# Latent attention with four heads' query columns in three weight units

## The reference

```python
q = (_rmsnorm(q_lat, g_q_lat[i]) @ w_q_up[i]).reshape(bsz, s, N_HEADS, QK_DIM)
kv = (_rmsnorm(kv_lat, g_kv_lat[i]) @ w_kv_up[i]).reshape(bsz, s, N_HEADS, NOPE_DIM + V_DIM)
q_nope, q_pe = q[..., :NOPE_DIM], q[..., NOPE_DIM:]
k_nope, v = kv[..., :NOPE_DIM], kv[..., NOPE_DIM:]
q_pe = _rope(q_pe, positions)
k_pe = _rope(k_rope[:, :, None, :], positions)
q_full = jnp.concatenate([q_nope, q_pe], axis=-1)
k_full = jnp.concatenate([k_nope, jnp.broadcast_to(k_pe, (bsz, s, N_HEADS, ROPE_DIM))], axis=-1)
ob = _chunk_causal_attention(q_full, k_full, v).reshape(bsz, s, N_HEADS * V_DIM)
```

## Time and profile before

| | before |
|---|---|
| median of 3 runs | 1703.1 us (1702.91 to 1703.26) |
| profiled execution | 1703.2 us |
| its span | 1701.4 us |
| mean granted TensorE clock | 0.997 of full |

### The profile page before, as it was taken

How to read it: one execution, slowest core, us unless ns; L and a number is a source line. 1 busy time by engine, 2 the same in 40 slices (tenths; PEclk the granted TensorE clock), 3 DMA queues, 4 the chain that set the end, 5 groups by cost and what they waited for, 6 DMA issues and landing times.

```text
span 1701.4 us, 22070 instructions
## 1 busy us (share of the span) xinstructions
PE 1687.1 (99%) x7852; PEld 1403.8 (83%) x7852; DVE 951.1 (56%) x1637; ACT 610.5 (36%) x1160; POOL 974.8 (57%) x595
## 2 busy tenths in 40 slices
PE   9999999999999999998999999999999999999998
PEld 8788888888888888887888888888888888888887
DVE  7877422156642554155767454438657967775244
ACT  5455311243221222144733322322523137765022
POOL 6656566665666666754755555546564663333654
PEclk9999999999999999998999999999999999999999
DMA  5222222222222222223222222222232221111222
GB/s 209 83 70 79 91 95 99 99 88 99 91 104 103 99 99 99 99 99 99 87 87 75 75 89 97 75 74 87 87 107 75 100 87 50 50 51 62 88 91 82
DMA packets 52424, 152.26 MB, mean 89 GB/s; under 512 B 11376, under 2 KB 12528, under 8 KB 52336
## 3 DMA queue, kind: packets, MB, share of 16 engines
q1 hardware_dynamic: 51472, 149.50, 25.5%
q10 hardware_dynamic: 864, 1.57, 0.3%
HBM read 148.95 MB, written 2.10 MB: 89 GB/s over the span
## 4 chain that ended last, share of the span: by engine, by line
PE 97%; DVE 2%; issue 1%; ACT 0%; POOL 0%; DVEq 0%; POOLq 0%
PE bank L867 28%; PE bank L868 28%; PE bank L869 28%; PE bank L1716 1%; PE bank L1314 1%; PE bank L1315 1%; PE bank L1318 1%; PE bank L1556 1%; PE bank L1555 1%; PE bank L1559 1%; PE bank L905 1%; PE bank L1053 1%; PE bank L891 0%; PE bank L1211 0%; DVE fx L2542 0%
## 5 line engine op out<-in xcount | busy, mean ns | idle before, releaser
L782 POOL TENSOR_SCALAR w_hi<-raw 128x1024 fp32r<-128x1024 f32 (+2 forms) x276 | 286.7, 1039 | 651.2 <-issue 480.1
L784 POOL TENSOR_TENSOR w_lo<-raw,w_hi 128x1024 fp32r<-128x1024 f32 (+2 forms) x276 | 645.6, 2339 | 23.1
L867 PE MATMUL bank<-op_hi,w_hi 128*128 128x512 f32 x964 | 381.7, 396 | 2.5 <-POOL w_lo L772 1.0
L869 PE MATMUL bank<-op_hi,w_lo 128*128 128x512 f32 x964 | 375.8, 390 | 0.0
L868 PE MATMUL bank<-op_lo,w_hi 128*128 128x512 f32 x964 | 375.5, 390 | 0.0
L867 PE MATMUL bank<-r,w_hi 128*128 128x512 f32 x856 | 339.1, 396 | 0.6 <-POOL w_lo L784 0.5
L869 PE MATMUL bank<-r,w_lo 128*128 128x512 f32 x856 | 333.9, 390 | 0.0
L868 PE MATMUL bank<-r,w_hi 128*128 128x512 f32 x856 | 333.7, 390 | 0.0
L867 PEld LDWEIGHTS bank<-op_hi,w_hi 128*128 128x128 f32 x964 | 181.3, 188 | 40.8 <-issue 2.2
L869 PEld LDWEIGHTS bank<-op_hi,w_lo 128*128 128x128 f32 x964 | 180.9, 188 | 38.1
L868 PEld LDWEIGHTS bank<-op_lo,w_hi 128*128 128x128 f32 x964 | 181.2, 188 | 36.0 <-issue 1.0
(11 more groups left out here) (310 smaller groups left out, 2335.2 us busy)
## 6 DMA issues: line engine op xcount, KB each, us to landing
raw<-in_weights SPq DMA_DIRECT2D x266, 512.0 KB, 3.2
out<-h SPq DMA_DIRECT2D x8, 256.0 KB, 2.0
h<-in_x SPq DMA_DIRECT2D x3, 512.0 KB, 7.9
raw<-in_weights SPq DMA_DIRECT2D x8, 192.0 KB, 2.4
raw<-in_weights SPq DMA_DIRECT2D x8, 128.0 KB, 2.5
cst<-in_consts SPq DMA_DIRECT2D x1, 832.0 KB, 11.3
raw<-in_weights SPq DMA_DIRECT2D x3, 256.0 KB, 3.1
rope_cos<-in_p ACTq DMA_DIRECT2D x3, 256.0 KB, 3.6
```

The costliest lines, as they stand in the source:

```text
L782: pool.tensor_scalar(hi, raw[:, r, at:w], 1.0, 0.0, ALU.mult, ALU.add).then_inc(hi_ready, 1)
L784: pool.tensor_tensor(lo, raw[:, r, at:w], hi.bitcast(F32), ALU.subtract).then_inc(split_ready, 1)
L867: pe.matmul(o, ah, bh, start=start, stop=False, skip_group_check=skip)
L869: return pe.matmul(o, al, bh, start=False, stop=stop, skip_group_check=skip)
```

## The change

Of four heads' query columns (4 x 96 = 384) three units of 128 columns are made in place of four. A pair unit `h0` holds head 0's nope columns and the rope columns of heads 0 and 2; `h1` holds head 1's nope columns and the rope columns of heads 1 and 3; `h2` holds the nope columns of heads 2 and 3. `h3` is gone; `h4` to `h7` go the same way. Each unit is put together by several loads with narrower columns, from the eight heads' weights in memory, which are stored as before.

Head 2's tile is head 0's, in which only the nope rows are replaced; its rotated rows are there already, rotated together with head 0's in one instruction of 64 rows. So that head 0's scores don't see head 2's rows, the query tile is multiplied by a column of ones and zeros (`head_rows`) when its high part and rest are made; five small memsets set the four columns at the start. The shared rotated key is copied to the rows 32 to 63 and 96 to 127, two copies on VectorE behind `kr_rot`; ScalarE's `k0h` waits for them.

```diff
-STAGES = [("lat", 6), ("attn", NH + 3 * JC + 2), ("mix", 3 * KD), ("wo", KD), ("res1", 1),
+STAGES = [("lat", 6), ("attn", NH - 2 + 3 * JC + 2), ("mix", 3 * KD), ("wo", KD), ("res1", 1),
...
-    if int(x[1:]) < (NH if x[0] == "h" else 3 * JC)]
+    if int(x[1:]) < (NH if x[0] == "h" else 3 * JC) and not (x[0] == "h" and int(x[1:]) % 4 == 3)]
...
+    def there(op, off):
+        n = 2 * p + off
+        return (n % 4 < 2 if op in ("ss", "qc", "sw", "qa") else off % 2 == 0 or n % 4 == off if op == "qf" else True)
...
-        rrows = (slice(0, 32), slice(64, 96))
+        rrows = (slice(0, 64), slice(64, 128))
+        unused_rows = (slice(32, 64), slice(96, 128), slice(0, 32), slice(64, 96))
+
+        def head_rows(n):
+            return st[:, n % 4:n % 4 + 1]
...
+                    query, key = slice(0, 3), slice(3, 5)
+                    if n % 2:
+                        columns(0, n, 0, NOPE + ROPE, query, landed[r])
+                        columns(NOPE + ROPE, n + 2, NOPE, ROPE, query, queries_in)
+                        return
+                    columns(2 * ROPE, n, 2 * ROPE, NOPE, slice(0, 5), landed[r])
+                    if n % 4:
+                        columns(0, n + 1, 0, NOPE, slice(0, 5), keys_in)
+                    else:
+                        columns(0, n, 0, ROPE, query, keys_in)
+                        columns(ROPE, n + 2, 0, ROPE, query, keys_in)
+                        columns(0, n + 1, 0, NOPE, key, keys_in)
...
-                if n % 2 and n > 1:
-                    pe.wait_ge(d.sem, d.at(f"kl_{n}"))
+                if n % 4 == 2:
+                    pe.wait_ge(d.sem, d.at(f"qa_{n - 1}"))
                 elif n > 1:
-                    pe.wait_ge(d.sem, d.at(f"qa_{n - 1}"))
+                    pe.wait_ge(d.sem, d.at(f"kl_{n - 1 + n % 2}"))
...
-                mla_query(y)
+                if p % 2 == 0:
+                    mla_query(y)
                 conv_unit(c, 0, 1)
...
-                hi(a, f"qf_{n}", mla_query_tile(n % 2), ps[0][:, :])
+                rows = krows[n % 2] if n % 4 > 1 else slice(0, P)
+                hi(a, f"qf_{n}", mla_query_tile(n % 2)[rows, :], ps[0][rows, :])
...
-                act.wait_ge(d.sem, d.at(f"qa_{n}"))
+                if n % 4 < 2:
+                    act.wait_ge(d.sem, d.at(f"qa_{n}"))
+                else:
+                    act.wait_ge(a.sem, a.at(f"qf_{n}"))
                 if n:
                     act.wait_ge(z.sem, z.at(f"s3_{n - 1}"))
-                hi(a, f"qh_{n}", aq_hi[:, 0], mla_query_tile(n % 2))
+                a.done(act.activation(aq_hi[:, 0], mla_query_tile(n % 2), ACT.Copy, scale=head_rows(n)), f"qh_{n}")
...
-            act.wait_ge(lat_d.sem, lat_d.at("kr_rot"))
+            act.wait_ge(lat_d.sem, lat_d.at("kr_96"))
...
+                if p % 2 == 0:
+                    mla_query_in(y + 2)
...
+            clear(st[:, 0:4], 1.0)
+            for n, rows in enumerate(unused_rows):
+                clear(st[rows, n:n + 1])
...
             add(d, "kr_rot", kr, kr, tmp)
+            sync(d, "kr_rot")
+            for first in (ROPE, 3 * ROPE):
+                d.done(dve.tensor_copy(kr[first:first + ROPE, :], kr[first - ROPE:first, :]), f"kr_{first}")
             mul(d, "rs2", rs_square, rs, rs)
...
-                lo(d, f"ql_{n}", aq_lo[:, 0], mla_query_tile(n % 2), aq_hi[:, 0])
+                stt(d, f"ql_{n}", aq_lo[:, 0], mla_query_tile(n % 2), head_rows(n), aq_hi[:, 0].bitcast(F32), ALU.mult, ALU.subtract)
```

More of the change, by code:

```diff
@@ L56 @@
 LOADS = _n
-UNITS = LOADS - 1
+UNITS = LOADS + 1
 RAW = 4
@@ L85, in attn_period @@
 def attn_period(table, p):
-    names = [(op, p + off, JC) if op[0] == "c" else (op, 2 * p + off, NH) for op, off in table]
+    def there(op, off):
+        n = 2 * p + off
+        return (n % 4 < 2 if op in ("ss", "qc", "sw", "qa") else off % 2 == 0 or n % 4 == off if op == "qf" else True)
+    names = [(op, p + off, JC) if op[0] == "c" else (op, 2 * p + off, NH) for op, off in table if there(op, off)]
     return [f"{op}_{n}" for op, n, end in names if n < end]
@@ L619, in load_attn, with columns @@
                 if name[0] == "h":
-                    u = U0["attn"] + int(name[1:])
-                    sp.dma_start(raw[:, r, 0:3 * P], ins["weights"][u, :, 0:3 * P]).then_inc(landed[r], 16)
-                    if int(name[1:]) % 2 == 0:
-                        for b in range(2):
-                            o = VD * (1 - b)
-                            head = ins["weights"][u + b, :, 3 * P:5 * P].rearrange("p (k n) -> p k n", k=2)
-                            keys = raw[:, r, 3 * P:5 * P].rearrange("p (k n) -> p k n", k=2)
-                            sp.dma_start(keys[:, :, o:o + VD], head[:, :, o:o + VD]).then_inc(keys_in, 16)
+                    n = int(name[1:])
+                    blocks = raw[:, r, 0:5 * P].rearrange("p (k n) -> p k n", n=P)
+                    def columns(at, head, first, width, some, done):
+                        source = ins["weights"][U0["attn"] + head, :, 0:5 * P].rearrange("p (k n) -> p k n", n=P)
+                        sp.dma_start(blocks[:, some, at:at + width], source[:, some, first:first + width]).then_inc(done, 16)
+                    query, key = slice(0, 3), slice(3, 5)
[10 more added lines that the diff above has]
+                        columns(0, n + 1, 0, NOPE, key, keys_in)
                     return
@@ L702, in _, with load_rounds @@
                 elif u < U0["mix"] + 6:
-                    load_from(U0["mix"] - 2 + first_columns[u - U0["mix"]], u % RAW)
+                    load_from(U0["mix"] + first_columns[u - U0["mix"]], u % RAW)
                 else:
-                    load_from(u - 2, u % RAW)
-            def load_rounds(first, rounds, ahead=2):
+                    load_from(u, u % RAW)
+            def load_rounds(first, rounds, behind=0):
                 with sp.Fori(first, rounds) as k:
@@ L711, in load_rounds, with load_single @@
                         sp.wait_ge(split_ready, k * RAW + (r - RAW + 1))
-                        load(k * RAW + (r - ahead), r)
+                        load(k * RAW + (r + behind), r)
+            def load_single(u):
+                if u == gla_up_unit:
+                    load_rank(u + 1, u % RAW)
+                else:
+                    load_from(U0["res1"] + 1 if u == U0["res2"] else u + 1 if u in (*range(U0["up0"], U0["res2"]), gla_low_unit)
+                              else u - 2 if u == gla_up_unit + 1 else u, u % RAW)
             def load_round(k):
@@ L716, in load_round @@
                     sp.wait_ge(split_ready, u - RAW + 1)
[L717 to L721 removed]
+                    load_single(u)
             load_rounds(first, U0["up0"] // RAW)
@@ L732, in _ @@
                 sp.wait_ge(split_ready, u - RAW + 1)
-                load_gla(GLA_UNITS[u - U0["gla"]], u % RAW)
+                if U0["gla"] <= u < U0["ln1"]:
+                    load_gla(GLA_UNITS[u - U0["gla"]], u % RAW)
+                else:
+                    load_single(u)
             load_rounds(gla_rounds, rounds)
@@ L741, in _ @@
                 else:
-                    load_from(u - (1 if u >= U0["ln2"] else 2), u % RAW)
+                    load_from(u + (1 if u >= U0["ln2"] else 0), u % RAW)
             end = S[ORDER[-1]]
@@ L755, in _ @@
             pairs = [attn_unit(f"h{n}") for n in range(0, NH, 2)]
-            queries = [attn_unit(f"h{n}") for n in range(1, NH, 2)]
+            queries = [attn_unit(f"h{n}") for n in range(1, NH, 4)]
             def missing(u):
@@ L2562, in _, with clear @@
             zeroed = [0]
-            def clear(x):
-                dve.memset(x, 0.0).then_inc(cleared, 1)
+            def clear(x, value=0.0):
+                dve.memset(x, value).then_inc(cleared, 1)
                 zeroed[0] += 1
@@ L2727, in mla_bank_rope @@
             def mla_bank_rope(step, n):
+                if n % 4 > 1:
+                    return
                 rows = rrows[n % 2]
```

37 lines of the change are left out of this document (18 added, 19 removed).

## The result

The changed kernel is slower: 1708.4 us median of eight executions (1706.9 to 1710.6) against 1703.2 (1702.9 to 1704.6) for the kernel before, ratio 1.0029, 95% interval 1.0020 to 1.0038. The prediction was 1703.3, that is +0.2, with a range up to 1705.6; measured were +5.2, and the time lies 2.8 us above the end of the range. The profiled execution took 1706.9 us (span 1705.1), 3.7 more than the one of before. It is the fastest of the eight; the slowest took 3.6 us more.

A forecast was written before the change was run, and what follows sets the result against it. TensorE's queue plus its holes was taken to bound the kernel. Gain 0.36 + 0.36 us from removed matmuls, loss 0.9 from the copies: +0.2 on the profiled 1703.2, median 0.1 lower, so 1703.3 us; range 1700.6 to 1705.6.

The forecast's parts named there:

- The wait at `s2`: Second and fourth periods: without the query unit TensorE waits for mask `m0`; of 2.16 us, 1.8 become wait, 0.36 gain.
- The wait for `vl3`: TensorE ahead of the first `s0`: wait for VectorE's `vl3` grows from 0.3 to 1.2 to 2 us.
- face value: Rival, second and fourth periods: removed matmuls save their full 2 x 2.16 = 4.3 us; time 1699.8; chance 0.12.
- that VectorE reach `m0` earlier: Condition for the full 4.3 us gain: `m0` comes before TensorE needs it, only if VectorE's backlog shrank.
- The term of the copies: VectorE's chain ahead of the first `s0`: two key copies lose 0.9 us, ends 0.5 and 2.9; `vl3` ends about 68.4.
- `ql_0`, which was put at nothing: Query-rest step on VectorE: three-operand `ql` takes +0.07 us, judged at `ql_2` to cost nothing, with 0.2 us to spare.
- The fourth period repeats it: 0.36 again: Fourth period: `m0` ends at 160.72, `s2` began at 161.14, so 0.36 us gain as in the second period.
- GpSimd would take the convolution's split earlier: GpSimd, free of `h3`'s split, takes the convolution unit's split earlier than before; stated against splits being late.
- the new holes slow TensorE's clock: Rival, first `s0` and each `s2`: half speed costs 2.5 us per fall, 7.5 at three holes (1710.8); all holes, chance 0.05.
- the late split: Rival: convolution unit's split ends after 95.50, costing up to 2 us, 1705.4; chance 0.08 together with one clock fall.
- a granted clock under 1.0 between 60 and 190 us: Sign in the attention stage that, if seen, would show the prediction wrong.
- rival B: From the experiments, not the prediction: copies and plain waits make the loss, the clock falls once at most; no chance given.

The follow-up runs named there:

- t5: Changed kernel with key rows doubled late (end of first period) and three more convolution blocks ahead of `s2` in periods two and four: 1699.12 us against 1703.94 before.
- e1: Kernel before plus only the two copies of the rotated key's rows behind `kr_rot`, `k0h` waiting for them: 1704.93 us against 1703.19 before.
- e4: Changed kernel with three more convolution blocks ahead of `s2` in the second and fourth periods, copies left in place: 1702.81 us against 1703.19 before.
- l7: Changed kernel with key rows doubled late and VectorE's `m0` ahead of `cc`, no convolution blocks moved: 1703.13 us against 1703.41 before.

## Why the prediction was wrong, step by step

**What held.** The wait at `s2`, by its mechanism, its releaser and in the second period its size: 1.63 us where 1.8 were forecast. `s2` came 0.36 us earlier behind the end of period 1, just as forecast (102.65 - 98.63 against 99.73 - 95.35), and 0.29 of it were left at the end of the period. The wait for `vl3`: 1.97, inside "1.2 to 2 us"; the wait for the split ahead of it fell from 1.0 to 0.5, as forecast. Nothing came from the extra `qf`, the 64-row rotations, the finer loads or the memsets: no wait for them in the list above. The removed matmuls have nearly their face value where other matmuls cover the chain to `m0` (`t5`: 2.13 and 1.75 us). The prediction had seen one other condition only, that VectorE reach `m0` earlier, and did not think of covering it.

**The term of the copies was too small.** Forecast 0.9 us, the row `vl3` to be at 68.4. Measured 1.25 for the copies (`e1`), and 0.3 for `ql_0`, which was put at nothing; `vl3` ended at 69.17. The turns of the copies themselves were right: they ended 2.2 us behind `kr_rot`, forecast and measured. The next three instructions were too cheap: `rs2`, `k0l` and `k1l` were to end at 59.0, 4.5 behind `kr_rot`, and ended 4.85 behind it in `e1` (4.84 in the changed kernel), so up to there the loss was 1.42 in place of 1.06. The 0.2 us that I guessed to come back behind them did come back, 0.17 in `e1`. The rest of the miss is `ql_0`: I looked at `ql_2`, which has cover, and not at `ql_0`, which stands in the one chain without cover.

**The fourth period isn't a repetition of the second.** "The fourth period repeats it: 0.36 again" turned out as -0.27. `clo` took 1.24 us there (0.69 before), beside a split of the full 1024 columns. In the kernel before GpSimd started this split 5.3 us behind the end of the third period (162.10 against 156.77), in the changed one 0.4 us behind it; with `h7` gone it has one unit less to split ahead of it. That the split stretched `clo` is read from their overlap; no run moved the split alone. VectorE before, then VectorE and GpSimd after:

```profile
159.15 0.69 DVE L2539 TENSOR_TENSOR r<-fx,r 128x512 fp32r<-128x512 f32 x1
```

```profile
162.15 1.24 DVE L2575 TENSOR_TENSOR r<-fx,r 128x512 fp32r<-128x512 f32 x1
```

```profile
160.15 2.69 POOL L810 TENSOR_TENSOR w_lo<-raw,w_hi 128x1024 fp32r<-128x1024 f32 x1
```

The prediction wrote that GpSimd would take the convolution's split earlier and counted that as a comfort only. It also brought the split beside the chain of `m0`. The wait became 2.03.

**The clock was the step that decided.** Copies, `ql_0` and the two periods make +1.5 us in place of +0.2, and would have left the time at 1704.7, inside the range. The step that failed is that the sum put the clock behind the new holes at nothing. That was the rival "the new holes slow TensorE's clock", to which I gave 0.08 for one fall (together with the late split) and 0.05 for all, and "a granted clock under 1.0 between 60 and 190 us" was one of the named signs of being wrong. Behind a hole of 1.97 or 1.98 us ahead of `s0` the clock fell in six of seven profiled executions; behind one of 2.03 to 2.06 in the fourth period in two of four; behind 1.6 in the second in none of four; behind the 0.3 ahead of `s0`, with 1.0 before it, in one of four changed or control kernels and not in the profile of before. The argument against it, that the holes stand between full queues and are only half as long as the stretch of the earlier trace rows, was no argument: nothing in the trace of before showed a hole of 2 us behind which the clock held. I had one case with a fall and none without, and took that as evidence for the latter. On the other hand a fall is cheaper than I said: 1.57 us, not 2.5.

By these counts the changed kernel loses 0.86 x 1.57 + 0.5 x 1.6 = 2.1 us to falls and the one before perhaps 0.3, so the sum is 1.5 + 1.8 = 3.3. Measured were 3.9 on one chip and 5.2 in the first comparison. But both profiled executions of the changed kernel were the fastest of their group. The mean clock counts all: 0.995 in seven of its seventeen executions, 0.996 in five and 0.997 in five, on the average 0.9959; before, 0.9975. The difference is worth 5.7 us at half clock (an estimate, 0.00166 x 1705 x 2), or 1.7 falls of 3.4 us, or 2.6 us of time, and 1.5 + 2.6 = 4.1 lies near what was measured. One fall in every execution, the most that rival B allows, would give 1.5 + 1.6 = 3.1. This is no proof: the same working gives `e1` 1.25 + 1.15 = 2.4 us where 1.7 were measured, so it is good to some 0.7 us. It can't tell either where in an execution the clock fell, since the stretch at 774 us counts in it as well. And TensorE's first block behind the opening starts between 9.91 us (`e4`) and 12.30 (`l7`), and at 10.25 and 11.12 in the two profiles of the changed kernel, so it varies with the execution too. What made the slowest execution of 1710.6 us is open; its mean clock is 0.995.

**The range.** One fall gave 1705.8 by my own working, and the range ended at 1705.6. With one unknown whose sign is known, at three places, and 2.5 us a piece by my own price, it had to reach to at least two falls, 1708.3.

## What to carry to other kernels

Taking work out of the queue of the engine that is the bound is worth its time only if something covers the chain that the work had hidden; here three blocks of independent matmuls moved in front of the waiting one, and the copies taken out of the chain, turned +0.3% into -0.26%; the same move of the blocks cost 0.2% in the kernel that still had the work. A hole of 2 us on TensorE costs its own length and, in many executions, 1.6 us of slow clock behind it: price a hole at both. And look at the one chain that nothing covers first: two small copies there cost more than eighteen matmuls gave, and the copies could be made some 28 us later without touching it.

## What the chip showed that I had not expected

The same program with the same holes to 0.03 us keeps or loses TensorE's clock from one execution to the next, at either hole, and each fall has nearly the same price, 1.55 to 1.65 us, from matmuls at 1.2 in place of 2.4 GHz. Where other matmuls fill the hole, the fall behind it is gone. An instruction added to VectorE beside GpSimd's splits costs by turns, not by its length: one copy +1.19 us, two +1.25, four +1.95, with 0.41 for a free one.
